# Two token tiles computed against both whole expert tables instead of by gathered rows, in a one-core hybrid encoder kernel on Trainium2

## What is computed

```python
def _peer(h, wq, subkeys, u, v):
    ...
        s1, i1 = lax.top_k(sc[:, :, 0], PEER_TOPK)
        s2, i2 = lax.top_k(sc[:, :, 1], PEER_TOPK)
        ...
        best, sel = lax.top_k(cand, PEER_TOPK)
        idx = jnp.take_along_axis(cidx, sel, axis=-1)
        g = jax.nn.softmax(best, axis=-1).astype(tb.dtype)
        ue = jnp.take(u, idx, axis=0)
        ve = jnp.take(v, idx, axis=0)
        a = jax.nn.gelu(jnp.einsum("thkd,td->thk", ue, tb), approximate=False)
        return jnp.einsum("thk,thkd->td", g * a, ve)
```

## The kernel before

| | before | after |
|---|---|---|
| second span: score begins | 264 | 264 |
| third span: inputs begin | 354 | 353 |
| attend begins | 407 | 383 |
| merge begins | 567 | 474 |
| out begins | 636 | 513 |
| score begins | 648 | 520 |
| dense work ends | 735 | 607 |
| first builds | 737 to 833 | 620 to 663 |
| first chunk, last chunk | 835, 1044 | 663, 834 |
| last `u` gather, last `v` gather | 1055, 1095 | 799, 839 |
| steps in which `v` is gathered | 40 to 583, 840 to 1095 | 40 to 839 |

## Time and profile before

### The profile page before, as it was taken

One profiled execution on the slowest core, in us unless ns is written; L12 is line 12 of the kernel. 1 busy time (PEld: TensorE's weight loads), 2 busy tenths in 40 slices (PEclk: granted clock), 3 DMA queues, 4 the chain that ended last, 5 costly groups with the idle time before them and its releaser, 6 DMA issues.

```text
span 4108.4 us, 41007 instructions
## 1 busy us (share of the span) xinstructions
PE 3191.7 (78%) x13101; PEld 1812.2 (44%) x13101; DVE 2504.3 (61%) x6368; ACT 917.2 (22%) x1918; POOL 2166.0 (53%) x1892
## 2 busy tenths in 40 slices
PE   8989978867779974668767777986533699888994
PEld 5667554534345432234534444543333533463331
DVE  2133255577766555656478776756999954696542
ACT  1245112244431110112134433211112200121000
POOL 1000034666656547756567766434655566676664
PEclk9999988977779986789877778998755599958996
DMA  6442487999999989989999999877977699989998
GB/s 217 122 148 92 141 291 283 391 335 367 363 342 411 368 340 355 392 320 386 352 337 363 372 349 367 326 264 247 331 274 233 209 401 420 418 288 352 419 420 321
DMA packets 520902, 1306.97 MB, mean 318 GB/s; under 512 B 47120, under 2 KB 243280, under 8 KB 520688
## 3 DMA queue, kind: packets, MB, share of 16 engines
q0 software_dynamic: 267264, 973.20, 62.9%
q1 hardware_dynamic: 213024, 289.45, 20.2%
q10 hardware_dynamic: 40400, 41.70, 3.1%
HBM read 1252.15 MB, written 52.02 MB: 317 GB/s over the span
## 4 chain that ended last, share of the span: by engine, by line
PE 41%; DVE 21%; DMA 15%; issue 9%; DVEq 5%; ACT 3%; POOL 3%; another core or an unknown queue 2%; SPq 1%; ACTq 0%; POOLq 0%
PE scores L889 7%; DVE G_u_rows L2125 7%; DMA G_v_rows<-in_peer_v,G_idxT 7%; PE scores L1773 6%; PE y_sum L2298 5%; PE scores L1777 4%; PE scores L2395 4%; PE scores L1555 3%; PE scores L1967 2%; PE scores L1462 2%; DMA T_chunks<-in_peer_v 2%; PE scores L1862 2%; PE o L1497 2%; POOL G_v_rows L765 1%
## 5 line engine op out<-in xcount | busy, mean ns | idle before, releaser
L765 POOL DMA_INDIRECT G_u_rows<-in_peer_u,G_idx x1056 | 1259.6, 1193 | 960.1 <-DVE G_dots L2125 530.4
L2125 DVE CUSTOM_DVE_ANT_0 G_u_rows<-G_u_rows,G_h 128x1024 f32<-128x1024 f32 x1056 | 1269.1, 1220 | 352.2 <-DMA G_u_rows<-in_peer_u,G_idx 300.7
L765 POOL DMA_INDIRECT G_v_rows<-in_peer_v,G_idxT x800 | 891.7, 1115 | 564.8 <-PE y_sum L2298 325.2
L2298 PE MATMUL y_sum<-G_v_rows,G_zw 128*32 128x512 f32 x3200 | 503.1, 758 | 170.0 <-DMA G_v_rows<-in_peer_v,G_idxT 144.1
L2395 PE MATMUL scores<-T_chunks,T_spread_w 128*128 128x512 f32 x1024 | 466.7, 610 | 26.9 <-DMA T_chunks<-in_peer_v 24.3
L2395 PEld LDWEIGHTS scores<-T_chunks,T_spread_w 128*128 128x128 f32 x1024 | 193.0, 194 | 301.4 <-issue 245.0
L2298 PEld LDWEIGHTS y_sum<-G_v_rows,G_zw 128*32 128x32 f32 x3200 | 100.8, 127 | 444.8 <-issue 440.3
L889 PE MATMUL scores<-A_w_in,A_hT 128*128 128x256 f32 (+2 forms) x864 | 225.8, 422 | 31.1 <-DMA A_w_in<-in_w_in 22.8
L722 POOL MEMSET G_zw<- 128x1024 f32 x2 | 1.9, 964 | 397.1 <-SPq L684 397.1
L889 PEld LDWEIGHTS scores<-A_w_in,A_hT 128*128 128x128 f32 x864 | 171.3, 201 | 85.2 <-DMA A_w_in<-in_w_in 23.3
L1480 PE MATMUL turn<-ident,C_probs 128*128 128x128 f32 x635 | 133.6, 327 | 94.8 <-ACT C_pT L1588 68.8
(11 more groups left out here) (314 smaller groups left out, 4648.7 us busy)
## 6 DMA issues: line engine op xcount, KB each, us to landing
T_chunks<-in_peer_v SPq DMA_DIRECT2D x64, 1024.0 KB
A_w_in<-in_w_in SPq DMA_DIRECT2D x24, 1024.0 KB
D_w_gate<-in_w_gate SPq DMA_DIRECT2D x24, 1024.0 KB
G_u_rows<-in_peer_u,G_idx POOLq DMA_INDIRECT x1056
G_v_rows<-in_peer_v,G_idxT POOLq DMA_INDIRECT x800
DF_w<-in_w_gate SPq DMA_DIRECT2D x12, 1024.0 KB
DF_w<-in_peer_wq SPq DMA_DIRECT2D x12, 1024.0 KB
F_w_q<-in_peer_wq SPq DMA_DIRECT2D x12, 1024.0 KB
```

Of the source, the lines that this page charges most:

```text
L765: pool.indirect_dma_start(out=buf[:, :], out_offset=None, in_=table, in_offset=bass.IndirectOffsetOnAxis(ap=rows, axis=0)).then_inc(signal ...
L2125: dve.tensor_tensor_reduce(out=self.u_rows[slot][:, :], in0=self.u_rows[slot][:, :], in1=self.h2[t % 2][:, :], scale=1.0, scalar=0.0, op0= ...
L2298: last = pe.matmul(self.ps_y[32 * c:32 * (c + 1), cols], self.zw[b % 2][:, lo:lo + 32], self.v_rows[self.ring_v.slot[4 * quad + c]][:, col ...
```

## The change

Tiles 4 and 5 leave the gathers altogether (`DENSE` = places 5 and 6). The gathered groups fall from 66 to 50, the `u` gathers from 1056 to 800; the `v` gathers stay 800. The two tiles' groups are still ranked, as an extra group beside each gathered one in groups 17 to 24 and 33 to 40 (`EXTRA`), and their keys and gates are kept.

After the dense work, for each of the 128 chunks of 128 experts:

- `turn_u`: the chunk of `peer_u` is transposed on PE in two halves of four transposes, each copied by ACT (512 columns) to `T_uT`;
- `dot_u`: eight matmuls of 256 columns give the products of 128 experts with the 256 tokens (`T_pairT`, the two tiles' rows transposed once), ACT takes the Gelu of 256 columns into `T_gz`;
- `weight_chunk`: DVE multiplies `T_gz` with the chunk's weights `T_spread_w`;
- `sum_v`: four matmuls of 512 columns with `peer_v`, as `chunk` before, but with `T_gz` as weights.

The weights are now built in three ranges of 43, 43 and 42 chunks (`RANGES`), so there are 96 builds of 8 matmuls with 43 columns. The `u` chunks have three buffers, the `v` chunks two, of 512 KB each, and SP loads each by itself. The step at which POOL fills the table of counts now waits for the third span's merge stage.

```diff
-STREAMED = (5, 6)
+DENSE = (5, 6)
+GATHERED = [at for at in range(TILES) if at not in DENSE]
+EXTRA = {FIRST[3 * (at // 3)] - 1 + h: (at, ORDER[at], h) for at in DENSE for h in range(HEADS)}
+DENSE_READY = [max(n for n, g in EXTRA.items() if g[0] == at) * TOPK + TOPK for at in DENSE]
+RANGES = ((0, 43), (43, 86), (86, 128))
+U_CHUNKS, V_CHUNKS = 3, 2
+LAST_CHUNK = 835
...
+        for r, (lo, hi) in enumerate(RANGES):
+            late += [("build", s, r, g) for s in range(len(DENSE)) for g in units if r or s]
+            for c in range(lo, hi + 1):
+                if c < hi:
+                    late.append(("turn_u", c, 0))
+                if sums < dots - 1:
+                    late.append(("sum_v", sums))
+                    sums += 1
+                if c < hi:
+                    late.append(("turn_u", c, 1))
+                if c > lo:
+                    late.append(("dot_u", dots))
+                    dots += 1
...
+            if c >= U_CHUNKS:
+                eng.wait_ge(self.t_turned, self.turn_no["turn_u", c - U_CHUNKS, 1] + 1)
...
+            if c >= V_CHUNKS:
+                eng.wait_ge(self.t_summed, c - V_CHUNKS + 1)
...
+        elif kind == "turn_u":
+            for b in range(4):
+                last = pe.transpose(bank[:, P * b:P * (b + 1)], self.u_chunks[slot][:, P * (4 * j + b):P * (4 * j + b + 1)], self.ident[:, :])
+        elif kind == "dot_u":
+            for b in range(DC):
+                last = pe.matmul(bank[:, 0:PAIR], self.uT[c % 2][:, b, :], self.pairT[:, b, :], start=(b == 0), stop=(b == DC - 1))
+        elif kind == "sum_v":
+            pe.wait_ge(self.t_weighted, c + 1)
+            pe.wait_ge(self.t_v[slot], 16 * (c // V_CHUNKS + 1))
...
+            act.activation(self.gz[c % 2][:, :], self.ps_2[self.bank[item]][:, 0:PAIR], ACT.Gelu).then_inc(self.t_gelued, 1)
...
+    def weight_chunk(self, dve, c):
+        dve.wait_ge(self.t_gelued, c + 1)
+        dve.tensor_tensor(gz[:, :], gz[:, :], self.spread_w[:, c - RANGES[r][0], :], ALU.mult).then_inc(self.t_weighted, 1)
```

More of the change, by code:

```diff
@@ new lines, in stream_at @@
+        late, dots, sums = [("turn", 1)], 0, 0
+        for r, (lo, hi) in enumerate(RANGES):
[11 more added lines that the diff above has]
+                    dots += 1
@@ new lines, in stream_at @@
+        late += [("sum_v", c) for c in range(sums, CHUNKS)]
+        cost = {"turn_h": 0.5, "turn": 0.5, "build": 1.8, "turn_u": 0.45, "dot_u": 1.7, "sum_v": 1.7}
+        first, turn = max(self.dense_end, DENSE_READY[0]) + 1, max(self.dense_end, DENSE_READY[1]) + 1
+        items = [(first + n * (turn - first) // len(early), item) for n, item in enumerate(early)]
+        spent = list(itertools.accumulate([0.0] + [1.0 if k < U_SLOTS else 0.5 for k in range(turn, LAST_CHUNK)]))
+        total, sofar = sum(cost[item[0]] for item in late), 0.0
@@ new lines, in stream_at @@
+        for item in late:
+            at = spent[-1] * sofar / total
+            items.append((turn + sum(x <= at for x in spent) - 1, item))
+            sofar += cost[item[0]]
+        for s in range(len(DENSE)):
+            items += [(LAST_CHUNK + 1 + 3 * s, ("finish", s)), (LAST_CHUNK + 3 + 3 * s, ("norm", s))]
+        self.stream, self.turn_no, self.build_no, self.bank, self.bank_after = {}, {}, {}, {}, {}
+        used = [None, None]
+        for step, item in items:
+            self.stream.setdefault(step, []).append(item)
+            if item[0] == "build":
+                self.build_no[item] = len(self.build_no)
+            bank = {"turn_h": item[-1] % 2, "turn": 0, "build": len(self.build_no) % 2, "turn_u": 0, "dot_u": 1}.get(item[0])
+            if bank is not None:
+                self.bank[item], self.bank_after[item], used[bank] = bank, used[bank], item
+            if item[0] in ("turn_h", "turn", "build", "turn_u"):
+                self.turn_no[item] = len(self.turn_no)
@@ L605, in stream_at, with range_of @@
         self.builds = list(self.build_no)
-        self.built = [1 + max(n for tick, n in self.turn_no.items() if tick[0] == "build" and tick[2] == half) for half in range(HALVES)]
+        self.built = [1 + max(n for item, n in self.turn_no.items() if item[0] == "build" and item[2] == r) for r in range(len(RANGES))]
+    def range_of(self, c):
+        return next(r for r, (lo, hi) in enumerate(RANGES) if c < hi)
     def ticks(self):
@@ L2115, in experts_dve @@
         yield
-        finish = {tile_end(at) + 2: at for at in range(TILES) if at not in STREAMED}
+        finish = {tile_end(at) + 2: at for at in GATHERED}
         for k in range(STEPS):
@@ L2355, in stream_dve @@
             s, = at
[L2356 removed]
+            x1 = self.v_chunks[s]
             dve.wait_ge(self.t_finish, 3 * s + 2)
```

465 lines of the change are left out of this document (249 added, 216 removed).

## The result

The changed kernel takes 4552.3 us (median of 4 runs, 4542.7 to 4560.6) against 4110.5 (4097.6 to 4120.5, 4 runs on the same chip): 1.108 times the time before, with a 95% interval of 1.103 to 1.112. Forecast were 4560 us and a range of 4270 to 4740. The profiled execution has a span of 4558.8 us.

The account below looks back on a forecast made before the run. Transfers pace most of the kernel before; after the change PE bounds the last stage. Dense work ending at 2935 us plus a last stage of 1615 us gave 4550 us of span, 4560 as a median, range 4270 to 4740.

Parts of the forecast that it names:

- I cost that at nothing: Up to step 353, about 1790 us: ranks added on DVE are hidden by transfers; without that cover, about 100 us.
- Attend, 340: Third span's attend, 91 steps instead of 160: 340 us, ends 290 and 420, from 272 us of attention and 60 of quads.
- The first 50 steps, 135: Start of the last stage, after the dense work, with 16 builds: paced by 100 gathers, 52 MB, 135 us.
- Chunks, 8.06 us each: Last stage, PE's work a chunk: sum 3.57 us, dots 3.51, eight transposes 1.0; 1031 us for 128.
- Emptying and refilling, 30: Last stage: pipeline of turns, dots and sums at three range starts, about 10 us each; 30 us, ends nothing and 60.
- Builds, 3.65 each: Last stage: 80 builds at 3.65 us of PE at the lower 1.2 GHz clock, 292 us; 190 if the clock stayed up.
- rival of shrinking stages: Third span's dense stages shrink with their steps at the pace before: dense work ends at 2660, kernel 4280 us; 12%.
- late stream: Chunk stage: `v` loads through two buffers come late, about 10.5 us a chunk, 310 us more, 4870 us; 10%.
- A new wait: nobody on the path should wait: Chunk stage: DVE's product waits for ACT's Gelu, which waits for PE's dots; no cost expected, 128 us if DVE came 1 us late each time.
- the lower clock: Chunk stage: PE runs at 1.2 GHz as in the builds, 16.1 us a chunk, 1031 us more, 5590 us; 5%.
- transfers bound the last stage: Not-slower rival: transfers, not PE, bound the last stage, which takes 890 us; ends at about 3830, 7% faster; 3%.
- they don't shrink at all: Third span's dense stages: the attention chain holds its pace, dense work ends at 3075 us, kernel 4700; 8%.

Follow-up runs that it names:

- before_later_last: The kernel before the change with its last chunk planned at step 1066 instead of 1046: 4050.1 us against 4043.0.
- half_bytes: Changed kernel with gathers of 512 instead of 1024 columns after each buffer's first use, products scaled by 1/64: 4455.2 us.
- short_product: Changed kernel with DVE's products of gathered `u` rows over 256 instead of 1024 columns, all transfers kept: 4513.5 us.
- half_dots: Changed kernel with 4 instead of 8 dot matmuls of 256 columns a chunk: 4333.4 us, 1.055 times the kernel before.
- half_turns: Changed kernel with two of the four transposes of each half chunk left out: 4496.0 us, 1.096 times the kernel before.
- least_u: Changed kernel with one transpose of four a half chunk and one dot matmul of eight a chunk: 4216.9 us, 1.027 times the kernel before.
- least_u_three_v: least_u with three instead of two buffers for `v` chunks: 4115.6 us, 1.018 times the kernel before on that chip.
- no_u_loads: Changed kernel loading only the first three chunks of `peer_u` and using them again and again: 4561.9 us, 1.112 times the kernel before.
- light: Changed kernel with gathers of half the bytes, products of 256 columns and quads of 64 columns together: 4325.6 us.
- short_quads: Changed kernel with 64 instead of 512 columns in all quads but a tile's first and last, all transfers kept: 4473.8 us.

## Why the prediction came out right, point by point

The mechanism was right: PE bounds the last stage, and the dense stages give almost nothing back. The sum was right to 8 us, but that nearness is luck. The dense stages ended 44 us later than forecast and the last stage was 35 us shorter, and the 8 us added for a median above the profiled execution went the other way (4552.3 for 4560.6).

- **Steps up to the third span, "I cost that at nothing".** At the out stage of the second span the changed kernel is 1.7 us later than the one before (1424.1 for 1422.4), and at the first matmul of the third span's inputs 16 us (1806 for 1790.5). The ranks added from step 272 on stand between the two. On the third chip it is about 21 us (1785.5 to 1786.9 in three kernels for 1765.1 in before_later_last). Small against the bound of 100 us that I gave, but not nothing. No run took them away there, so that they are the cause is only argued.
- **Inputs, 205.** 197 us.
- **Attend, 340: the term that was mis-sized.** 410 us, near the upper end of 420. The working had the right parts: 272 us of attention and 60 of quads make 332, and the trace has 333.8 with 62.9 of quads. I then wrote that the stage "won't run at the sum of PE's busy time" and added only 8 us for it. The gaps are 76. The trace of before had a hint. Of the 128 us that PE was idle in its attend, 68 were waits for attention's own results:

```profile
PE turn L1480 <- ACT C_pT L1588: 49.2, 20, 13.9
PE scores L1462 <- DVE C_ntop L1646: 19.1, 8, 4.8
```

  332 and 68 make 400, an estimate that would have been near. half_bytes and short_product show that neither the transfers nor DVE's products alone set this time; for the quads it is open, since the clock fell with them.
- **Merge, 225, and out, 75.** 209 and 59: merge at PE's limit, at clock 1.00, out with PE busy for 53.5 of 60 us.
- **Score, 300.** 298, at DMA share 0.95. With half the bytes it is still 282, so something else stands just behind the transfers. The step "this is where half of the gain goes back" holds: 180 us before.
- **End of the dense work, 2935.** 2979: 70 too little in attend, 16 at the start, 42 too much in the other stages.
- **The first 50 steps, 135.** 164. The bound was named rightly, its bytes weren't: 61 MB at 371 GB/s.
- **Chunks, 8.06 us each.** 7.8. I had taken lengths of rows; by the starts of the rows that follow, each part is a few per cent shorter, since the pipelined end of a row lies over the next (3.60 long, 3.44 from start to start). half_dots and half_turns give 1.70 us for half of the dots and 0.44 for half of the transposes, by the clock on the wall. 128 chunks at 7.8 us are 1000 of the 1106 us of the three ranges, 37 quads 1.85 each, another 68.
- **Emptying and refilling, 30.** No row of before had this term. The rest of the three ranges is 1106 - 1000 - 68 = 38 us, with four builds among it (7.9 us). At the first range start PE waits 0.69 us for ACT's copy three times in a row, and its transposes, four in 1.11 us, are still at the lower clock.
- **Builds, 3.65 each.** 3.42. Before, builds of 64 columns at the lower clock came 3.58 us apart (3658.13 to 3661.71 us in the earlier trace rows):

```profile
3593.78 3.62 PE L2402 MATMUL turn<-T_hot 128*128 128x43 f32 x16
3597.19 3.62 PE L2402 MATMUL o<-T_hot 128*128 128x43 f32 x16
3600.60 3.62 PE L2402 MATMUL turn<-T_hot 128*128 128x43 f32 x16
```

  3.41 us from start to start, at clock 0.51 to 0.58. So most of the 0.24 us comes from the columns, and the rest from a row's length taken for its period. "43 columns for 64 save nothing" was nearly right: they save about 5%. What the builds pay for is the clock. Before, one in the middle of them ran at the full clock:

```profile
3640.36 1.95 PE L2382 MATMUL turn<-T_hot 128*128 128x64 f32 x16
```

  In the changed kernel, too, the first two builds after a chunk range take 1.98 us (3564.67 and 3568.43 us); then PE waits 4.65 us for ACT's copy, and the builds that follow are at the lower clock although PE is busy for 111.9 of the stretch's 116 us. 76 builds at 3.42 instead of 1.98 are an estimated 110 us. No run tried to get them back.
- **The end, 25.** 21.
- **The signs.** The chunk stage came out as the sign of being right asked, with PE busy 98 to 100%, clock 0.98 to 0.99 and DMA share 0.64 to 0.69, and so did score. Attend (340), the end of the dense work (2935), chunk to chunk (8 to 8.5) and the builds (3.7) were each missed.
- **Slips in the working.** 182 gathers and 12 MB in attend are 107 MB, which at the 353 GB/s of that stage is 305 us and not 290; as attend took 410, it changes nothing. Seven steps of out at 7 us are 49 and not 30, so the rival of shrinking stages stands at 4300. In the late stream, by its two buffers alone, a load of 15 us and a sum of 3.57 for every two chunks make 9.3 us a chunk and not 10.5, so 160 us more and not 310: 4720, which is inside the range of 4270 to 4740 and not outside it.
- **"A new wait: nobody on the path should wait".** From the page: DVE does wait for ACT, and PE's dots and sums wait for neither.

```profile
L2416 PE MATMUL o<-T_pairT,T_uT 128*128 128x256 f32 x2048 | 466.8, 381 | 0.0
L2425 PE MATMUL scores<-T_v_chunk,T_gz 128*128 128x512 f32 x1024 | 466.0, 598 | 0.0
L2473 DVE TENSOR_TENSOR T_gz<-T_gz,T_spread_w 128x256 f32<-128x256 f32 x128 | 54.4, 425 | 836.7 <-ACT T_gz L2460 828.9
```

  828.9 us of waiting on DVE cost nothing, since it waits for the slow engine's work to come round. The queue behind it takes it too: `u` gathers wait 840.1 us for DVE and `v` gathers 896.5 for PE over the span, and all of them still end with the chunks.

Of the rivals, the lower clock fell by the clock of 0.98 to 0.99, with eight transposes in every chunk. The Trainium skill, TensorE: Matmul & The Clock Gate, Part 4: PE-mode transpose, has it that the full clock doesn't engage for transposes. Mixed with float32 matmuls as they are here it did, at 0.98 to 0.99, and half_turns says that fewer of them don't raise it (0.97). The late stream fell by the 0.0 idle in front of L2425; it stands behind PE, and two buffers cost some 65 to 70 us once PE's work is cut (least_u, least_u_three_v). That the dense stages shrink with their steps fell with attend. That transfers bound the last stage fell with a DMA share of 0.64 to 0.69 and with no_u_loads. That they don't shrink at all came nearest, in attend alone.

## What to carry to other kernels

Before moving work to an engine, look at how full that engine is in the stage where the work will stand, not over the span: PE was at 78% in all, but at 90% from 3270 to 4015 us, where the chunks stood. It had 266 us of idle time in the whole last stage before, and has 122 now; PE's work there grew by 625 us and the stage by 482. Work taken out again (half_dots) came back one for one. A stage that is paced by a shared resource and also has a chain of its own gives back, at most, the difference between the two when the resource is relieved. Estimate the chain's time first, by adding to PE's busy time only the waits for the stage's own results. In a sum of rows that lie back to back, take the time from start to start, not the rows' lengths.

## What the runs showed of the hardware

- **The clock can fall when work is taken out.** With shorter quads, attend's clock fell from 0.80 to 0.66, and PE's busy time rose from 333.8 to 354.8 us although 46 us of quad work were gone; light shows the same (0.67). The other matmuls of the stage took 67 us more. These are one run each, but not a slow chip: in the same run of short_quads merge had 0.99 and the first chunk range 0.96. The quads woven into attention thus did more than use its gaps.
- **A gather has a price on POOL that doesn't depend on its bytes.** In light, whose gathered rows are half as long, two gathers that follow each other:

```profile
2599.99 0.95 POOL L797 DMA_INDIRECT G_u_rows<-in_peer_u,G_idx  x1 [0.30 <-issue]
2601.24 0.95 POOL L797 DMA_INDIRECT G_v_rows<-in_peer_v,G_idxT  x1 [0.30 <-issue]
```

  1.25 us for each gather of 128 rows, 0.95 and 0.30 between; with whole rows, in the changed kernel's score, 0.94 and 0.30. The transfer of a whole one takes 1.3 us at 400 GB/s, so halving the bytes can gain next to nothing where POOL issues without a pause. Many issues take longer: the mean of a `u` gather is 1.12 us in the changed kernel and 1.13 with half the bytes, but 0.97 in short_product, where DVE's products are a quarter as long. So it goes with DVE's work beside it and not with the bytes; why is not shown.
- **Float32 transposes at the full clock take 0.11 us each**, back to back in fours (0.43 to 0.44 us), between matmuls of 3.45 us.
